# Layer 0's expert-row gathers: weights taken up in another order on PE, over seven places instead of six

## What is computed

```
def _peer(h, w_pq, peer_keys, peer_down, peer_up):
    q = (h @ w_pq).reshape(B, L, PEER_HEADS, 2, PEER_QDIM // 2)
    s = einsum("blhpd,hpkd->blhpk", q, peer_keys)
    ...                                   # top 16 of 128 twice, top 16 of their 256 sums
    eidx = take_along_axis(cidx, pos, -1) # 8 heads x 16 = 128 experts a token
    gate = softmax(top_s, axis=-1)
        a = einsum("tkd,td->tk", peer_down[ee], hh)
        act = gg * gelu(a)
        return einsum("tk,tkd->td", act, peer_up[ee])
```

## Time and profile before

| | us |
|---|---|
| median of 3 runs | 3848.91 |
| lowest, highest | 3846.46, 3853.41 |
| the profiled execution | 3838.83 |
| its span, first to last instruction | 3837.0 |
| layer 0's gathers in it, first issue to last up | 367 to 1925 |
| layer 1's gathers in it | 2070 to 2735 |

### The profile page before, as it was taken

How to read it: one execution, slowest core, us unless ns; L and a number is a source line. 1 busy time by engine, 2 the same in 40 slices (tenths; PEclk the granted TensorE clock), 3 DMA queues, 4 the chain that set the end, 5 groups by cost and what they waited for, 6 DMA issues and landing times.

```text
span 3837.0 us, 44307 instructions
## 1 busy us (share of the span) xinstructions
PE 3174.7 (83%) x15370; PEld 1938.4 (51%) x15370; DVE 2396.1 (62%) x5191; ACT 1605.2 (42%) x4579; POOL 743.1 (19%) x797
## 2 busy tenths in 40 slices
PE   5898977888896875767778877777799989999899
PEld 2485533233351231122346432333397879898798
DVE  3444678555568777454455887786665866565564
ACT  1432455565555555655542111112233533334433
POOL 0000233233323323333301333333200000000000
PEclk8998998899897887888989989999999989999999
DMA  7665999999999998999925999999754235454454
GB/s 292 271 252 212 343 396 393 356 393 407 409 393 379 388 368 347 407 402 413 418 96 225 396 402 420 401 413 415 295 186 171 93 121 195 165 197 170 142 175 154
DMA packets 163870, 1158.01 MB, mean 302 GB/s; under 512 B 18785, under 2 KB 19553, under 8 KB 26978
## 3 DMA queue, kind: packets, MB, share of 16 engines
q0 software_dynamic: 110592, 805.36, 51.7%
q1 hardware_dynamic: 53090, 350.30, 25.0%
HBM read 1154.53 MB, written 1.05 MB: 301 GB/s over the span
## 4 chain that ended last, share of the span: by engine, by line
PE 54%; DVE 18%; DMA 17%; ACT 6%; issue 4%; POOL 0%; SPq 0%; DVEq 0%; POOLq 0%; ACTq 0%
PE ps L1304 9%; PE ps L1302 9%; PE ps L1303 9%; PE ps L1240 7%; DMA rows<-in_peer,diag 5%; PE ps L1210 4%; DMA h_ctx<-in_peer,idx 3%; PE ps L1159 3%; DMA rows<-in_peer,idx 3%; DMA wring<-in_peer,diag 3%; PE ps L1105 3%; PE ps L903 2%; DVE rows L2347 2%; PE ps L1131 2%; DVE shared L2557 1%
## 5 line engine op out<-in xcount | busy, mean ns | idle before, releaser
L2347 DVE CUSTOM_DVE_ANT_0 rows<-rows,ps 128x1024 f32<-128x1024 f32 x342 | 408.8, 1219 | 304.2 <-DMA rows<-in_peer,diag 228.6
L1240 PE MATMUL ps<-rows,diag 128*32 128x512 f32 x1368 | 413.7, 700 | 178.6 <-ACT diag L1815 175.8
L2825 POOL DMA_INDIRECT rows<-in_peer,diag x342 | 324.2, 948 | 1075.9 <-PE ps L1240 698.1
L1302 PE MATMUL ps<-hT_hi,w_hi 128*128 128x256 f32 x1792 | 508.0, 283 | 8.9 <-DVE hT_lo L2469 8.9
L1304 PE MATMUL ps<-hT_lo,w_hi 128*128 128x256 f32 x1792 | 508.7, 284 | 0.0
L1303 PE MATMUL ps<-hT_hi,w_lo 128*128 128x256 f32 x1792 | 506.9, 283 | 0.0
L1302 PEld LDWEIGHTS ps<-hT_hi,w_hi 128*128 128x128 f32 x1792 | 343.3, 192 | 14.4 <-issue 14.3
L2459 DVE TENSOR_TENSOR w_lo<-wring,w_hi 128x2048 fp32r<-128x2048 f32 x120 | 274.8, 2292 | 112.0 <-ACT w_hi L1874 110.2
L1303 PEld LDWEIGHTS ps<-hT_hi,w_lo 128*128 128x128 f32 x1792 | 342.6, 191 | 0.1
L1304 PEld LDWEIGHTS ps<-hT_lo,w_hi 128*128 128x128 f32 x1792 | 341.5, 191 | 0.0
L1210 PE MATMUL ps<-rows,diag 128*128 128x512 f32 x512 | 252.3, 644 | 80.2 <-ACT diag L1799 73.2
(11 more groups left out here) (355 smaller groups left out, 6226.2 us busy)
## 6 DMA issues: line engine op xcount, KB each, us to landing
wring<-in_wgu SPq DMA_DIRECT2D x66, 1024.0 KB, 4.9
wring<-in_wdn SPq DMA_DIRECT2D x33, 1024.0 KB, 4.9
wring<-in_wG SPq DMA_DIRECT2D x32, 1024.0 KB, 8.2
wring<-in_wmod SPq DMA_DIRECT2D x28, 1024.0 KB, 7.9
wring<-in_wpq SPq DMA_DIRECT2D x24, 1024.0 KB, 7.2
rows<-in_wgu SPq DMA_DIRECT2D x22, 1024.0 KB, 4.9
rows<-in_wmod SPq DMA_DIRECT2D x20, 1024.0 KB, 7.7
rows<-in_wdn SPq DMA_DIRECT2D x11, 1024.0 KB, 4.8
```

The costliest lines, as they stand in the source:

```text
L1240: ins = pe.matmul(ps[qd:qd + QUAD, UPB + half, :], quad_w[:, n % GROUP, :], spread_place(n)[:, D + half * 512:D + (half + 1) * 512], start ...
L1302: pe.matmul(out_, lh[l_at], rh[r_at], start=start, stop=False, skip_group_check=skip)
L2347: dve.tensor_tensor_reduce(out=down, in0=down, in1=h_ps, scale=1.0, scalar=0.0, op0=ALU.mult, op1=ALU.add, accum_out=a8[:, c:c + 1]).then_ ...
L2825: pool.indirect_dma_start(out=spread_place(n), out_offset=None, in_=A["peer0"], in_offset=bass.IndirectOffsetOnAxis(ap=idx_moved[t][:, col ...
```

## The change

- **Places.** A table gives each place the gathers that may use it; each gather takes the allowed place used longest ago. Gathers 0 to 23 have six places, 24 to 199 seven (the context's h lends one), 200 to 287 six, 288 to 511 seven (x itself lends one). POOL waits for the up of the gather before in the same place, and at a place's first use for the reader of what was in it.
- **x.** SP writes x to the output's memory once x0 is done (before the chunk of stage zA x1 0) and reads it back when the last gather in its place is taken up (before the chunk of stage gate x1 0 3); line 2244's stage waits for that in x1. The context's h is computed again only when gather 199 has been taken up (a wait of ACT); gate values of c0 that lay in it lie elsewhere.
- **PE's order.** In each half-group PE does the first up, then the stages with up to three more ups between their pieces, then what is left. `spread_h` for the next quarter stands right before the fourth up, wherever that falls.
- **Quarters to and fro.** Odd sets of heads run through the quarters backwards, so that 40 instead of 48 gathers begin a new quarter.
- **Stages.** pq 3 of x0 moves from half-group 0 to before `moved`, ahead of the first gather. kv 0 and kv 1 of x1 no longer share half-group 27: kv 0 to 3 take half-groups 27 to 30.

```diff
-SPREAD_PLACES = 6
-LENT = 166
+PLACES = {"rows0": (0, 511), "rows1": (0, 511), "rows2": (0, 511), "rows3": (0, 511), "x_ctx": (0, 167), "wring": (0, 511),
+          "h_ctx": (24, 199), "keys": (168, 511), "x_in": (288, 511)}
...
 def spread_gathers(t):
 
-    return [(TOP * h0 + QUADS * s + j, j, n) for n, (h0, h1) in enumerate(SETS[t]) for j in range(QUADS) for s in range(TOP * (h1 - h0) // QUADS)]
+    to_and_fro = range(QUADS), range(QUADS - 1, -1, -1)
+    return [(TOP * h0 + QUADS * s + j, j, n) for n, (h0, h1) in enumerate(SETS[t]) for j in to_and_fro[n % 2] for s in range(TOP * (h1 - h0) // QUADS)]
...
 def new_quarter(n):
-    return n % P == 0 or SPREADS[n][1:] != SPREADS[n - 1][1:]
+    return n % P == 0 or SPREADS[n][1] != SPREADS[n - 1][1]
+
+def spread_places():
+
+    where, before, use, last, used = [], [], [], {}, {}
+    for n in range(len(SPREADS)):
+        place = min((p for p, (lo, hi) in PLACES.items() if lo <= n <= hi), key=lambda p: last.get(p, -1))
...
 def scoring(r):
 
     first = routes(r, 0, (0, 8))
-    return [[("take", r)], [("pq", r, 0)], [("pq", r, 1)], first[0:4], [("pq", r, 2)], first[4:]]
+    return [[("take", r)], [("pq", r, 0)], [("pq", r, 1)], first[0:4], [("pq", r, 2)]] + [[("pq", r, 3)], first[4:]] * (r == "x0")
...
 def begin(r, slots):
 
-    slots[0] += [("pq", r, 3)] + [("pq", r, 4)] * (r == "x0") + routes(r, 0, (1,))
+    slots[0] += [("pq", r, 4 if r == "x0" else 3)] + routes(r, 0, (1,))
...
-    place(at, [k[5:7]] + k[7:])
+    place(at, k[5:])
...
             def ups_to(n):
                 while next_up[0] < n:
+                    k = next_up[0] + 1
+                    if k % HALF == 0 and k < len(SPREADS) and new_quarter(k):
+                        spread_h(k)
                     spread_up(next_up[0])
                     next_up[0] += 1
                     pieces[0] = 0
...
                     if n == 0:
                         spread_h(0)
-                    last_up[0] = n + HALF - 1
+                    ups_to(n + 1)
+                    last_up[0] = n + HALF
                     run_stages(stages)
-                    ups_to(n + HALF - 1)
                     last_up[0] = 0
-                    if n + HALF < len(SPREADS) and new_quarter(n + HALF):
-                        spread_h(n + HALF)
                     ups_to(n + HALF)
...
+                if (run, k) == ("c0", 1):
+                    act.wait_ge(upp_done, LAST_IN["h_ctx"] + 1)
...
-                if run == "c0":
-                    dve.wait_ge(ld_c, 32)
+                if run != "x0":
+                    dve.wait_ge(ld_c if run == "c0" else ld_x, 32)
...
+                if name == "zA" and args == ["x1", 0]:
+                    at_mark(sp, "fin", "x0", 2)
+                    sp.dma_start(out.rearrange("(t p) d -> p t d", p=P), x[0][:, :, :]).then_inc(x_kept, 16)
+                if name == "gate" and args == ["x1", 0, 3]:
+                    sp.wait_ge(upp_done, LAST_IN["x_in"] + 1)
+                    sp.wait_ge(x_kept, 16)
+                    sp.dma_start(x[0][:, :, :], out.rearrange("(t p) d -> p t d", p=P)).then_inc(ld_x, 16)
...
-                if n >= SPREAD_PLACES:
-                    pool.wait_ge(upp_done, n - SPREAD_PLACES + 1)
+                place, before = PLACE_OF[n], BEFORE_IN[n]
+                if before is not None:
+                    pool.wait_ge(upp_done, before + 1)
...
+                elif place == "h_ctx":
+                    pool.wait_ge(mm_done, mm_at["hT", "c0", 2, 1, 1])
...
+                elif place == "x_in":
+                    pool.wait_ge(mark["h"], h_mark("x1", 0, 2))
+                    pool.wait_ge(x_kept, 16)
```

More of the change, by code:

```diff
@@ L97, in spread_gathers @@
 def spread_gathers(t):
-    return [(TOP * h0 + QUADS * s + j, j, n) for n, (h0, h1) in enumerate(SETS[t]) for j in range(QUADS) for s in range(TOP * (h1 - h0) // QUADS)]
+    to_and_fro = range(QUADS), range(QUADS - 1, -1, -1)
+    return [(TOP * h0 + QUADS * s + j, j, n) for n, (h0, h1) in enumerate(SETS[t]) for j in to_and_fro[n % 2] for s in range(TOP * (h1 - h0) // QUADS)]
 SPREADS = [g for _ in range(2) for t in range(TT) for g in spread_gathers(t)]
 def new_quarter(n):
-    return n % P == 0 or SPREADS[n][1:] != SPREADS[n - 1][1:]
+    return n % P == 0 or SPREADS[n][1] != SPREADS[n - 1][1]
[3 more added lines that the diff above has]
+        place = min((p for p, (lo, hi) in PLACES.items() if lo <= n <= hi), key=lambda p: last.get(p, -1))
+        where.append(place)
+        before.append(last.get(place))
+        used[place] = used.get(place, 0) + 1
+        use.append(used[place])
+        last[place] = n
+    return where, before, use, last
+PLACE_OF, BEFORE_IN, USE_OF, LAST_IN = spread_places()
 def scoring(r):
     first = routes(r, 0, (0, 8))
-    return [[("take", r)], [("pq", r, 0)], [("pq", r, 1)], first[0:4], [("pq", r, 2)], first[4:]]
+    return [[("take", r)], [("pq", r, 0)], [("pq", r, 1)], first[0:4], [("pq", r, 2)]] + [[("pq", r, 3)], first[4:]] * (r == "x0")
 def spread(slots, ranks, counts):
@@ L601, in gate_at @@
                 if n < 2:
-                    return h[1][:, 0, n * 512:(n + 1) * 512]
+                    return U[:, 9216 + n * 512:9216 + (n + 1) * 512]
                 if n in (2, 11):
@@ L606, in gate_at @@
                     return kT[:, 1, 2 * (n - 3):2 * (n - 2), :]
-                return vv[:, n - 5, :] if n < 9 else h[1][:, 1, (n - 9) * 512:(n - 8) * 512]
+                return vv[:, n - 5, :] if n < 9 else h[0][:, 0, (n - 9) * 512:(n - 8) * 512]
             if dp == 3:
@@ L619, in build @@
         both += [kvmem[:, n * 2 * D:(n + 1) * 2 * D] for n in range(3)] + [h[1][:, :, :].rearrange("p t n -> p (t n)")]
-        lent = x[1][:, :, :].rearrange("p t n -> p (t n)"), kvmem[:, 0:2 * D]
+        place_at = {f"rows{n}": both[n] for n in range(HALF)}
+        place_at.update({"x_ctx": x[1][:, :, :].rearrange("p t n -> p (t n)"), "x_in": x[0][:, :, :].rearrange("p t n -> p (t n)"),
+                         "h_ctx": both[GROUP - 1], "keys": kvmem[:, 0:2 * D], "wring": wring[:, SLOTS - 1, :]})
         at[0] = 0
@@ L675, in build @@
         chunk_in = [sem(f"chunk_in{n}") for n in range(SLOTS + ROW_SLOTS)]
-        row_in = [sem(f"row_in{n}") for n in range(SPREAD_PLACES)]
+        row_in = {p: sem(f"row_in_{p}") for p in PLACES}
         var_ready, rs_ready, half_set = sem("var_ready"), sem("rs_ready"), sem("half_set")
@@ L756, in spread_place @@
         def spread_place(n):
-            k = n % SPREAD_PLACES
-            return both[k] if k < HALF else lent[n > LENT] if k == HALF else wring[:, SLOTS - 1, :]
+            return place_at[PLACE_OF[n]]
         block = ctx.enter_context(nc.Block())
@@ L2818, in gather_spread @@
                     at_mark(pool, "moved", run, set_mark(t, set_))
[L2819 to L2826 removed]
+                place, before = PLACE_OF[n], BEFORE_IN[n]
+                if before is not None:
+                    pool.wait_ge(upp_done, before + 1)
+                elif place == "wring":
+                    pool.wait_ge(mm_done, max(chunk_done[m] for m in range(first_chunks()) if slots[m][0] == SLOTS - 1))
+                elif place == "h_ctx":
+                    pool.wait_ge(mm_done, mm_at["hT", "c0", 2, 1, 1])
+                elif place == "keys":
+                    pool.wait_ge(mm_done, mm_at[s_key("c0", H - 1, 0)])
+                elif place == "x_in":
+                    pool.wait_ge(mark["h"], h_mark("x1", 0, 2))
+                    pool.wait_ge(x_kept, 16)
+                pool.indirect_dma_start(out=place_at[place], out_offset=None, in_=A["peer0"],
+                                        in_offset=bass.IndirectOffsetOnAxis(ap=idx_moved[t][:, col:col + 1], axis=0)).then_inc(row_in[place], 16)
             def gather_both(t):
```

8 lines of the change are left out of this document (4 added, 4 removed).

## The result

The changed kernel takes 3923.85 us (median of 4 runs, 3920.49 to 3924.74), the kernel before, beside it on the same chip, 3847.68. The ratio is 1.0195 [1.0177, 1.0213]. The forecast was 3804.4, with 3854 as the upper end; the sign was wrong.

A forecast was written before the change was run, and what follows sets the result against it. Layer 0's gathers were taken as bound by a ring of waits leaving 113.3 of 1500 us without transfers. 0 + 24 + 19 + 4 - 2.5 = 44.5 us off 3848.9 gave 3804.4 us, range 3767 to 3854 (8 in 10).

The forecast's parts named there:

- The first half-groups: First four half-groups of layer 0's gathers, gather 0's to 16's product: 71.8 us falls to 57.7, 14 less.
- pq 3: Before the first gather: one more block of queries and its scores on PE delay that gather, cost 8.0 us.
- The claim on the context's h: Gather 24 waits for half-group 5's transposes, now behind its first up: cost 5 us, bounds 0 and 7.5.
- The deep holes: 667:767 and 1367:1567 us, 42.0 us missing: 24 won, 8 of 15.5 in the deepest (1504 to 1522) and 16 elsewhere.
- the other holes: Rest of 667:767 and 1367:1567: ups and spread behind all of PE's stages; 16 of 26.5 us won.
- The places: Stretches at 393 to 401 GB/s with seven places: reserve 2.6 transfers instead of 1.6, 19 of 34.1 us won.
- 967:1267: Stretch from 967 to 1267 us, 20.0 us missing, mostly six places: only the order can help, 4 us won.
- Fewer quarters: Eight spreads of 1.90 us leave PE, 15 us in all; effect already counted in the other shares.
- x out and back: x's write in a transfer-bound stretch costs 2.5 us, 5 at the upper end; the read back is hidden, 0.
- Slower: PE now waits first: Rival: 1.9 us of PE's stage work moves behind the weight in some 38 half-groups, 72 us, 3876 us; chance 0.12.
- a ring: Gathers' stretch: landing, DVE, ACT, PE, place free, POOL, landing wait on each other; none of PE, DVE, ACT is full.
- The share of HBM: Gathers' stretch: a core's HBM share, about 358 GB/s, would already bind and the change win nothing; within no effect's 0.09.

The follow-up runs named there:

- the fastest kernel: Changed kernel with PE's old order and pq 3 back in half-group 0, against the kernel before: 3810.40 us, ratio 0.9899 [0.9882, 0.9915].

## Why the prediction was wrong, point by point

**The first half-groups.** Forecast 71.8 to 57.7 us, measured 60.0 (383.2 to 443.2). PE bounds them, as forecast; the chain that ended last, changed kernel, has PE's items end to end there (start us, us, what):

```profile
410.98 1.93 PE ps L1180 x8
412.91 1.85 PE ps L1248 x16
414.76 0.86 PE ps L1261 x4
```

But the cause was wrong. With the *old* order the same stretch takes 56.2 (380.9 to 437.1), less than with the new. pq 3's block gone from it gives 8 of the 15.6 (64.1 with pq 3 back), and that block is paid ahead of the first gather; the rest came with the quarters to and fro (71.9 with the places alone): the second set begins in the quarter where the first ended, so gather 16 needs no spread. The order gave -3.8.

**pq 3.** Forecast +8.0 for the first gather and -8.0 inside the 14: net 0. First gather 9.7 later in the changed kernel (377.1 against 367.4), 7.6 by pq 3 alone; net 0 to 5. Right.

**The claim on the context's h.** Forecast 5. With the old order gather 24 is issued at 453.8 against 452.6: 1. With the new it is issued at 472.2, 19.6 late, and its product comes 10.3 late. PE's timeline there, changed kernel:

```profile
456.57 1.05 PE L1261 MATMUL ps<-x_ctx,diag 128*32 128x512 f32 x4 [2.25 <-ACT diag L1836]
...
467.28 1.05 PE L1261 MATMUL ps<-rows,diag 128*32 128x512 f32 x4 [2.30 <-ACT diag L1836]
468.27 3.63 PE L904 MATMUL ps<-ident,h_ctx 128*128 128x128 f32 x16
```

The transposes do stand right behind half-group 5's first up, as forecast, but that up comes at 467.28 and not at 459.4. Gather 16's product was at 443.2, its weight only at 456.5: ACT, which makes the weights in order with its other work, was waiting for the block of queries that PE ends at 453.4, with the ups of gathers 13 to 15 between its pieces. So the claim itself costs some 1 us, and what I mis-sized is the delay that the order had built up by then: the step assumed half-groups of 13.9 us, and this one took 21.1 (443.2 to 464.3).

**The deep holes.** The step on the deepest hole was right in kind and size. POOL's wait of at most 10 us and over 200 GB/s were forecast, 11.2 and 320 came, and of the 8 us given to it 8.0 came: from gather 364's product to 396's the changed kernel takes 88.8 us (1586.1 to 1674.9) where before it was 96.8 (1504.5 to 1601.3). The kv split has some 5 of them, more than its share in the forecast. The order by itself shrinks POOL's wait as well, to 11.2 us with six places and kv together, but that kernel takes 98.7 us from 364 to 396: a wait is not worth its length if what follows is slower. The 16 for the other holes is the step that failed: "ups and the spread behind all of PE's stages" was taken as the fault, while the stages ahead of the ups were what DVE and ACT were fed from.

**The places.** Forecast 19 in the stretches with seven and a share of the 24; measured 28 alone. By the products of gathers that is 12 us between 24 and 200 and 17 from 288 on, less 5 between 252 and 288. Issue to landing rose from 9.3 us to 9.9 in the changed kernel and to 10.8 with the old order, as it should where more gathers are in flight. With the old order 767 to 967 us runs at 408 for 401 and 1767 to 1867 at 421. Right in kind, and the size was set too low. 967:1267, given 4 by the order, got 387 for 391 with the old order and 328 with the new.

**Fewer quarters.** 640 records of `spread_h`, 40 x 16: as forecast. What they are worth in time no run shows, since none changes the quarters alone. From the places alone to the fastest kernel it is 9.5 us (3819.9 - 3810.4, two intervals that overlap, 0.9910 to 0.9954 and 0.9882 to 0.9915), which is quarters and split together, and the split has some 5 of it. The 7.8 us won in the first four half-groups are gone by gather 364 (1487.6 and 1488.2).

**x out and back.** Forecast: 2.5 lost. No run has it apart from the place; both together gain 16. The 5.0 us (places alone) and 7.6 us (fastest kernel) lost between gathers 252 and 288 say that the way out and the claim on the place cost more than the 2.5. The transfers took 4.9 us out and 5.8 back, issue to landing.

**The sum.** Without the order the rest brings 3848.0 - 3815.6 = 32 us, 38 with pq 3 left alone. The forecast was 44.5, but 16 of it (the other holes) and 4 (967:1267) were to come from the order, so the rest was forecast at some 24 and did better. The order was put at +20, and cost 108.

**The rival that was right.** "Slower: PE now waits first" named the mechanism, 38 half-groups x 1.9 = 72 us; the first up alone measured 74. That these two agree is in part luck: by the traces the first up alone adds 50 us between gathers 124 and 252, 1.5 in each of those 32 half-groups (2.9 in half-group 43), and 30 in the others, to which the rival gave next to nothing. Its time of 3876 was still 48 us under what came. It got 0.12 because of one sentence: "DVE does its four products before it needs the stage, which is three landings or 7.5 us later". That sentence failed. It takes the products to come at the pace of landings. In half-group 43 the rows had landed, the four took 4.6 us, and the first weight came 3.0 us after the first product began (949.44 to 952.42). PE's stage then began 4.3 us after the first product, when before it had begun 0.55 us ahead of it, so 4.8 us moved behind the wait where I had counted 1.9. The 1.9 was also the length of a piece of work at the clock's upper level and not of the wait: what counts is how long PE would have worked while the weight was made, and that the same work took longer afterwards (the granted clock of 0.51), which no case priced either. The rival's other gap was the early fourth up with its spread, 1.9 + 1.0 us between two pieces of a stage (45 us), which no case priced, though the sum counted its gain.

**Views that would have told it.** The earlier trace rows had both numbers side by side, PE waiting 266 us for the weight and POOL 698 for the up (1032 over all places, as DVE's 229 are 356), and I read them as a ring that an earlier up closes faster. PE's 193 waits say the opposite of so many of the 512 ups: there the weight was late and not the up's turn on PE, and putting the up earlier lengthens the wait. The rival said so ("it often meets the up too early"), and the timelines of PE and DVE side by side for one ordinary half-group, of which I had read only PE's (955 to 1000 us), would have shown PE's six products lying in the time in which the weight is made.

**The share of HBM**, weighed in the prediction as a bound, played no part: with seven places and the old order 100 us ran at 421 GB/s. The Trainium skill, Perfetto Trace Analysis ("Roofline"), allows a core that draws on its HBM alone about 120% of the 358 GB/s of its share, by an estimate from these two figures 430 GB/s. The trace agrees, at 118%; whether the neighbour was idle, no run shows.

## What to carry to other kernels

An instruction that waits belongs *behind* the work of its engine that does not wait: before moving one ahead, take the timeline of an ordinary period and see what the engine does in the time in which the awaited value is made. If two engines exchange work in both directions within a period, moving a release earlier on one of them is a gain only if the other's next input doesn't stand behind it. One more buffer in flight gave 28 us here with no such condition, and the deepest hole in the profile, once filled, gave back half of its 15.5 us while the new order cost 108 elsewhere: try the buffer first, and measure reorderings apart from it. When a buffer count changes, compare the waits over all buffers, since a line for one name then counts fewer transfers. And read a busy time that grows for the same work as a sign of the clock.

## What was not expected of the hardware

One core took 421 GB/s over 100 us of indirect gathers of 8 KB rows with up to seven in flight, against 419 with six: the rate at full was reached before, and the seventh place only made it last longer. And a reordering that adds no work made TensorE busy for 43 us more, with a granted clock of 0.51 right behind a wait of 4.45 us.
